# Attention's units reordered to sample, prompt, prompt, with the sample keys turned later and one value load issued earlier

## The reference

```
q = (h @ attn_w_q)                       # 3 groups x 8 heads x 64
for g, (window, dilation) in enumerate(((128, 1), (512, 4), (2048, 16))):
    logits = q[:, :, g] . keys[t - dilation * n] / 8 + bias[g][n]   # n <= window/dilation
    o[g], lse[g] = softmax over n, weighted values
y = merge of the three groups by softmax(lse)  @ attn_w_o
```

## Time and profile before

| what | value |
|---|---|
| median of 3 runs | 2262.54 us (2262.34 to 2266.04) |
| the profiled execution's own time | 2262.11 us |
| its span | 2260.2 us |
| mean granted TensorE clock | 0.992 |
| PE busy | 2214.9 us, 98% |
| DVE busy | 1617.6 us, 72% |
| ACT busy | 890.1 us, 39% |
| DMA, mean over the span | 135 GB/s |

### The profile page before, as it was taken

How to read it: one execution, slowest core, us unless ns; L and a number is a source line. 1 busy time by engine, 2 the same in 40 slices (tenths; PEclk the granted TensorE clock), 3 DMA queues, 4 the chain that set the end, 5 groups by cost and what they waited for, 6 DMA issues and landing times.

```text
span 2260.2 us, 41620 instructions
## 1 busy us (share of the span) xinstructions
PE 2214.9 (98%) x17636; PEld 2102.0 (93%) x17636; DVE 1617.6 (72%) x2138; ACT 890.1 (39%) x1167; POOL 137.3 (6%) x191
## 2 busy tenths in 40 slices
PE   7999999999999999999999999999999999999998
PEld 6999999987799999998889999999987789999998
DVE  7983995699789849953358956984445479947963
ACT  6431443222654314432234422442145555413442
POOL 0000000323010000001001000001001100000001
PEclk8999999999899999999999999999999999999999
DMA  5543443554244435423439533532959933233321
GB/s 156 158 151 110 151 156 93 164 141 126 72 147 150 140 100 164 153 83 90 132 107 304 173 114 99 168 115 73 240 148 281 253 113 94 75 98 96 88 77 55
DMA packets 372091, 305.61 MB, mean 135 GB/s; under 512 B 13798, under 2 KB 338414, under 8 KB 371050
## 3 DMA queue, kind: packets, MB, share of 16 engines
q1 hardware_dynamic: 365485, 232.06, 36.4%
q0 software_dynamic: 6464, 71.76, 9.2%
q10 hardware_dynamic: 12, 0.02, 0.0%
HBM read 284.45 MB, written 70.54 MB: 157 GB/s over the span
## 4 chain that ended last, share of the span: by engine, by line
PE 88%; DVE 6%; issue 2%; ACT 2%; DMA 2%; SPq 1%; DVEq 0%; ACTq 0%
PE ps L2101 34%; PE ps L2157 13%; PE ps L2159 13%; PE ps L2158 13%; PE ps L2565 2%; PE ps L2563 2%; PE ps L2564 2%; PE ps L2401 2%; PE ps L2609 1%; DMA kc<-in_cache_kv_w 1%; DVE blk L1572 1%; PE ps L2725 1%; DVE hlS L1549 1%; PE ps L2663 1%; PE ps L2716 1%
## 5 line engine op out<-in xcount | busy, mean ns | idle before, releaser
L1087 ACT CAST hlS<-blk 128x1024 fp32r<-128x1024 f32 x176 | 184.3, 1053 | 207.0 <-PE ps L2159 169.4
L2101 PE MATMUL ps<-actH,oWA 128*128 128x288 f32 x1408 | 250.4, 296 | 0.0
L2101 PE MATMUL ps<-actH,oWB 128*128 128x288 f32 x1408 | 250.0, 296 | 0.0
L1716 DVE SCALAR_TENSOR_TENSOR cs<-ps,rstd 128x576 f32<-128x576 f32 x64 | 48.5, 757 | 246.9 <-PE ps L2101 246.9
L1549 DVE TENSOR_TENSOR hlS<-blk,hlS 128x1024 fp32r<-128x1024 f32 x176 | 213.5, 1216 | 2.4 <-ACT hlS L1087 2.4
L2157 PE MATMUL ps<-tM,hlA 128*128 128x288 f32 x704 | 212.4, 302 | 2.9 <-DVE hlA L1549 2.4
L2157 PE MATMUL ps<-tE,hlS 128*128 128x288 f32 x704 | 208.5, 296 | 4.1 <-DVE hlS L1549 4.1
L2101 PEld LDWEIGHTS ps<-actH,oWA 128*128 128x128 f32 x1408 | 209.0, 189 | 1.2 <-DVE cs L1611 0.6
L2101 PEld LDWEIGHTS ps<-actH,oWB 128*128 128x128 f32 x1408 | 209.0, 189 | 0.0
L2157 PE MATMUL ps<-tM,hlS 128*128 128x288 f32 x704 | 208.2, 296 | 0.0
L2158 PE MATMUL ps<-tM,hlA 128*128 128x288 f32 x704 | 208.0, 295 | 0.0
(11 more groups left out here) (323 smaller groups left out, 5363.3 us busy)
## 6 DMA issues: line engine op xcount, KB each, us to landing
blk<-in_ffn_w_in SPq DMA_DIRECT2D x352, 256.0 KB, 4.1
raws<-in_ffn_w_out SPq DMA_DIRECT2D x64, 704.0 KB, 4.7
out_kv_sample<-in_cache_kv_w POOLq DMA_DIRECT2D x8, 4064.0 KB, 16.8
out_kv_sample<-in_cache_kv_w POOLq DMA_DIRECT2D x8, 2016.0 KB, 9.2
wst<-in_conv_w_pw SPq DMA_DIRECT2D x24, 512.0 KB, 4.1
wst<-in_w_kv SPq DMA_DIRECT2D x24, 512.0 KB, 3.8
kc<-in_cache_kv_w SPq DMA_DIRECT2D x40, 256.0 KB, 9.1
kc<-in_cache_kv_w SPq DMA_DIRECT2D x8, 1024.0 KB, 7.7
```

The source lines that it names most:

```text
L1087: nc.scalar.copy(o, a).then_inc(S["f_h"], 1)
L1716: nc.vector.scalar_tensor_tensor(px[m % 2], pair(2 + m % 2), 0.5, rstd[:], ALU.mult, ALU.mult).then_inc(S["px_ready"], 1)
L2101: nx = nc.tensor.matmul(outs[t], a, b[:, t, :], start=start and first, stop=stop and b is xh and not first)
```

## The change

- The unit order becomes sample, prompt, prompt: unit i is a sample unit where i % 3 is 0.
- ks (e, 0) is turned two slots ahead of the scores of sample unit e and ks (e, 1) with k0 one slot ahead (before: three, two and one). The loop starts at slot -2.
- The three groups of a pair's keys are turned in one slot, every sixth, which is a sample slot. Before they were spread over three slots.
- SP's waits and issues follow; `pair_bias` and `pair_values` come one slot later in their cycle of six.
- `pair_values(1)` is issued in the query projection instead of slot 2. For that `vinB` is placed in the last 4 blocks of the weight region, which the projection doesn't use.
- Behind the loop ACT waits for all units before it copies half 0, because the last unit is now a prompt unit, whose tokens lie in both halves.

The diff, cut to its core:

```diff
 def prompt_unit(i):
-    return divmod(i // 3 * 2 + i % 3, 4) if i % 3 < 2 else None
+    return divmod(i // 3 * 2 + i % 3 - 1, 4) if i % 3 else None
 def sample_unit(i):
-    return i // 3 if i % 3 == 2 else None
+    return None if i % 3 else i // 3
 def sample_keys_of(s):
-    e, x = divmod(s + 1, 3)
-    return (e, x) if e < NB else None
+    e, y = divmod(s + 2, 3)
+    return (e, y) if e < NB and y < 2 else None
 def prompt_keys_of(s):
-    j, g = divmod(s + 3, 6)
-    return (j, g) if 0 < j < PAIRS and g < 3 else None
+    j, y = divmod(s + 3, 6)
+    return j if 0 < j < PAIRS and y == 0 else None
...
+        pair_values(1)
...
         fresh_values(0)
-        for s in range(-1, UNITS + 3):
+        for s in range(-2, UNITS + 3):
             after = sample_keys_of(s)
             if after and after[0] + 1 < NB:
-                last = ("ks", *after, PAIRS - 1) if after[1] < 2 else ("k0", after[0])
-                sp.wait_ge(S["t_mm"], TURN[last][0] + 1)
+                sp.wait_ge(S["t_mm"], TURN["ks", *after, PAIRS - 1][0] + 1)
                 key_rows(after[0] + 1, after[1])
+                if after[1] == 1:
+                    sp.wait_ge(S["t_mm"], TURN["k0", after[0]][0] + 1)
+                    key_rows(after[0] + 1, 2)
...
-            elif s == 2:
-                pair_values(1)
             kp = prompt_keys_of(s)
-            if kp and kp[1] == 2 and kp[0] + 1 < PAIRS:
-                sp.wait_ge(S["t_mm"], TURN["kp", *kp][0] + 1)
-                pair_keys(kp[0] + 1)
+            if kp and kp + 1 < PAIRS:
+                sp.wait_ge(S["t_mm"], TURN["kp", kp, 2][0] + 1)
+                pair_keys(kp + 1)
...
         act.wait_ge(S["pv_mm"], UNITS - 1)
         split_high(CB["wo"], 0, SIZE["wo"])
-        act.wait_ge(S["o_evac"], UNITS - 1)
+        act.wait_ge(S["o_evac"], UNITS)
+        act.wait_ge(S["t_dve"], TURN["o", NB - 1][2])
         for k in range(PAIRS):
             nc.scalar.copy(oH[:, k, 0], oT[:, k, 0]).then_inc(S["h_h"], 1)
-        act.wait_ge(S["t_dve"], TURN["o", NB - 1][2])
-        act.wait_ge(S["o_evac"], UNITS)
         for k in range(PAIRS):
             nc.scalar.copy(oH[:, k, 1], oT[:, k, 1]).then_inc(S["h_h"], 1)
...
             ks, kp = sample_keys_of(s), prompt_keys_of(s)
-            if ks and ks[1] < 2:
+            if ks:
                 keys_sample(*ks, 0)
                 keys_sample(*ks, 1)
             if 0 <= s - 3:
                 values(s - 3)
-            if ks and ks[1] < 2:
+            if ks:
                 keys_sample(*ks, 2)
                 keys_sample(*ks, 3)
-            elif ks:
+            if ks and ks[1] == 1:
                 keys_dense(ks[0])
             if kp:
-                keys_prompt(*kp)
+                for g in range(3):
+                    keys_prompt(kp, g)
```

More of the change, by code:

```diff
@@ L246, in turn_table @@
         if kp:
-            order.append((("kp", *kp), "act"))
+            order += [(("kp", kp, g), "act") for g in range(3)]
         if 0 <= s - 3 and sample_unit(s - 3) is not None:
@@ L431, in trunk_program @@
                           place("oSs", [P, P]))
+    sbias = place("sbias", [P, SC])
     assert at[0] <= w_at
-    sbias, kTs, kT, vinB, bTB = (place("sbias", [P, SC]), place("kTs", [P, PAIRS, CN]), place("kT", [P, 2, 12, P]),
-                                 place("vinB", [P, 12, P]), place("bTB", [P, 2, PW]))
-    kfT = place("kfT", [P, PAIRS, 2 * FR])
+    at[0] = w_at
+    kTs, kT, bTB, kfT = (place("kTs", [P, PAIRS, CN]), place("kT", [P, 2, 12, P]), place("bTB", [P, 2, PW]),
+                         place("kfT", [P, PAIRS, 2 * FR]))
+    assert at[0] >= w_at + 18 * BLK * 4
+    vinB = place("vinB", [P, 12, P])
     assert at[0] <= w_at + 22 * BLK * 4
@@ L473, in probabilities @@
     def probabilities(i):
-        return sP[i % 3]
+        return sP[i % 3 - 1]
     def slot_column(x, r):
@@ L818, in _ @@
                 fresh_values(1)
-            elif s == 2:
-                pair_values(1)
             kp = prompt_keys_of(s)
-            if kp and kp[1] == 2 and kp[0] + 1 < PAIRS:
-                sp.wait_ge(S["t_mm"], TURN["kp", *kp][0] + 1)
-                pair_keys(kp[0] + 1)
-            if s >= 0 and s % 6 == 4 and s // 6 + 2 < PAIRS:
+            if kp and kp + 1 < PAIRS:
+                sp.wait_ge(S["t_mm"], TURN["kp", kp, 2][0] + 1)
+                pair_keys(kp + 1)
+            if s >= 0 and s % 6 == 5 and s // 6 + 2 < PAIRS:
                 sp.wait_ge(S["sm_ready"], s + 1)
                 pair_bias(s // 6 + 2)
-            if s >= 3 and (s - 3) % 6 == 4 and (s - 3) // 6 + 2 < PAIRS:
+            if s >= 3 and (s - 3) % 6 == 5 and (s - 3) // 6 + 2 < PAIRS:
                 sp.wait_ge(S["pv_mm"], s - 3 + 1)
@@ L1965, in bias_low @@
             else:
-                if i == 2:
+                if i == 0:
                     dve.wait_ge(S["sbias_in"], 16)
@@ L2675, in turn @@
                 if x == 0:
-                    pe.wait_ge(S["pn_ready"], i // 3 * 2 + i % 3 + 1)
+                    pe.wait_ge(S["pn_ready"], i // 3 * 2 + i % 3)
                 out, (_, r), t = bank_for(("p", i, x)), prompt_unit(i), probabilities(i)
```

## The result

The changed kernel takes 2270.03 us, the median of 8 runs (2264.36 to 2274.12), against 2264.91 us for the kernel before in 8 runs beside them (2262.34 to 2266.47). The ratio is 1.0026, with a 95% interval of 1.0017 to 1.0034: slower by some 5 us. The forecast was 2262.6 us and no change, with 2257.5 to 2268.5 as its range.

What follows compares the result with a forecast made beforehand. PE was taken as the bound (88% of the chain), with full DMA engines setting the middle's pace. Terms -0.6 + 2.1 - 1.4 - 1.9 + 2.1 = +0.3 us on 2262.11 gave 2262.6 us, range 2257.5 to 2268.5.

Steps and rivals of the forecast that it cites:

- start: First attention slots: k0's copy wait and its clock go, four smaller costs come; -0.6 us, bounds -1.9 and +0.7.
- middle slots: Middle sample slots: DVE's oSs copy lies bare, probability turns come late, kTs waits go; +2.1 us, bounds +0.5 and +3.5.
- waits for kc: PE's waits for key rows in the middle: 1.0 us instead of 2.4; -1.4 us, bounds -2.4 and +5.
- late instructions: PE's "issue" waits amid full DMA engines, with their clock: 2.7 us instead of 4.6; -1.9 us, bounds -4.6 and +2.
- end: Last units and start of wo: new 2.5 us wait plus clock, less old waits; +2.1 us, bounds -0.3 and +3.
- Two small doubts: At the start: the clock may fall again, 0.7 us; ACT's table load may delay a turn of keys, 0.3 us.
- The slower rival: First prompt slot's keys queue in SP behind pair keys and values, late in slots 7, 13, 19: 2271.9 us, chance 0.2.
- the wait at the squares: Behind wo, squares waiting for ACT behind the next feed-forward's first loads: 1.14 us mostly goes, 0.15 kept.
- The clock behind it: Behind the 2.5 us wait ahead of wo: lowered clock, three in four times 1.6 us, +1.2 us.

Runs made afterwards that it cites:

- thin values: Only 32 of 128 partitions of the 2048-window value rows loaded from sample unit 2 on: 2259.64 us in changed, 2256.84 us in before.
- thin pairs: Changed kernel, with keys of pairs 1 up and values and biases of pairs 2 up loading a quarter of their partitions: 2265.27 us.
- late load: Changed kernel with pair_values(1) issued in slot 2 again, as before: 2269.72 us.
- spread: Changed kernel with the pair values of pairs 2 and 3 issued two slots later, in slots 10 and 16: 2267.82 us.
- thin changed: Changed kernel with a quarter of the 2048-window value rows loaded from sample unit 2 on: 2259.64 us, ratio 0.9979.
- thin before: Kernel before with a quarter of the 2048-window value rows loaded from sample unit 2 on: 2256.84 us, ratio 0.9967.
- the thin pair: The changed kernel and the kernel before, both with the same value rows left out: 2259.64 and 2256.84 us.
- early split: Changed kernel with ACT's split of wo's first chunk two slots earlier: 2273.06, 2269.97 us; 2258.97 with fewer value rows, 2264.55 with sample keys turned as before.
- the best kernel with all its loads: Kernel before with ACT copying k0 ahead of its first exponential in slot 1: 2262.32 us, ratio 0.9992.

## Why the prediction was wrong

The ledger of the two profiled executions, step by step, in us; the measured terms are the waits of the lists above, with what the clock cost behind them:

| step | predicted | measured |
|---|---|---|
| start | -0.6 | -1.6 |
| middle slots | +2.1 | +2.2 |
| waits for kc | -1.4 | -2.4 |
| late instructions | -1.9 | +2.6 |
| end | +2.1 | +3.3 (about +2.1 in the other traces, see below) |
| sum | +0.3 | +4.1 (the executions differ by 4.0) |

**The start** was right in its parts: 0.77 for k0 (said 0.75), 1.53 for the bias (said 1.6). Two small doubts fell the good way: the 1.53 us wait didn't lower the clock (0.7), and no wait followed ACT's table load (0.3). -3.9 + 0.77 + 1.53 = -1.6.

**The middle** was right: four of the five oSs waits of 0.55 and three of 0.25 for kT, less 0.7 for kTs. 2.2 + 0.7 - 0.7 = +2.2.

**The waits for kc**: the profiled execution flatters. Over the traces of the unaltered kernels they are 1.5 us on average after (0, 1.1, 3.5) and 3.2 before (2.4, 4.0): -1.7, near the -1.4 forecast. The slower rival asked for waits of 5 us and more in slots 7, 13 and 19; changed itself shows none such, so the direction it warned of came about by another mechanism.

**The late instructions** are the step that failed: "The DMA stays full for much of the stretch, so I take 2.7 after: -1.9 us". They were taken to shrink with the bytes that left the stretch. The waits went from 3.3 to 5.7 us instead (+2.4), and with the clock the term is +2.6, 4.5 us from the forecast and beyond the upper bound of +2 that I had given it. The clock's part hardly moved: about 1.3 before by the prediction's count, about 1.5 after, where the granted clock is 0.59 at 1748 to 1752. All three traces of the unaltered changed kernel have 5.7 to 5.9 us. What the runs show of the cause:
- It needs full DMA engines: taking bytes away cuts it to 1.9 us (thin values) and 3.4 us (thin pairs) in this order, and to 0.3 in the old order.
- It isn't the early load (late load: 4.8), nor the bunched issues alone (spread: 2.7, but kc 9.1).
- It has a place. Of the waits in slot 12's sample values the profiled execution has 3.3, its repeats 2.5 and 2.5, the late load 3.1 and the thin kernel 1.9 us. Before, the one of 2.4 us stands in the values of a sample unit too.

The traces say what PE waits for. The 18 traces here hold 68 "issue" waits of PE in attention (of more than 0.15 us), and each ends 1.3 to 1.7 us behind the end of a load of 16 KB on DMA queue q8, of the kind "instruction". Counting PE's products and weight loads together, in order, PE resumes each time at a number that differs from the others by a multiple of 256, give or take one (25844, 26100, 26356, 26612, 27123, 27891 and 28403 in changed). Attention has 4836 of them in changed, 18.9 times 256, and 19 of these loads, in every one of the 18 traces. So an "issue" wait is a block of 256 instructions that comes late. The long one, with the block before it and the wait itself (columns as in the earlier trace rows), and then the queues from 1743.5 to 1744.7 (packets, MB, share of 16 engines):

```profile
1737.95:1742.94 4.99, 4.99 (x129) 3.36 (x128) 2.66 (x6) 2.00 (x5) 0.58 (x1) 1.00 1.05 255
1742.94:1746.23 3.29, 0.00 (x1) 0.00 (x0) 0.00 (x0) 0.00 (x0) 0.00 (x0) 1.00 1.07 314
```

```profile
q1 hardware_dynamic: 215, 0.42, 100.0%
q8 instruction: 1, 0.02, 5.6%
```

PE went through the block before (129 products, 128 weight loads) in 4.99 us. The load of the next one started 5.57 us after that block had begun, took 1.07, and PE went on 1.64 us behind it: 8.28 us, less the 4.99 of work, is the wait of 3.29. Over nine blocks of the middle the load starts on average 5.1 to 5.2 us into the block before in the three traces of changed, 4.7 and 4.8 in the two of before, 3.3 and 2.4 in thin changed and thin before. So these loads start late when the engines are full, and nearly as late before as after. With the new order they come some 0.4 us later, and the quickest of the nine blocks takes PE 5.0 us of work instead of 5.5. There are seven such waits in each trace of changed and two in each of before. How much of the +2.4 is the load and how much the quicker blocks isn't separated. The prediction had the term hang on the crowding alone, and left out the other side, how soon PE is through a block. Why a load starts that late is not shown beyond its going with the amount of data; that it queues behind the data is the reading that fits.

**The end**: the wait of 2.46 us was foreseen at 2.5, with its chain, and the wait at the squares went as foreseen. The clock behind it was forecast at 0.75 x 1.6 = 1.2. From the first product of wo to the first one of the squares are 12.37 us, against 9.78 before (1821.40 to 1832.32 less the 1.14 us wait): 2.6 us. The term: 2.5 + 2.46 + 2.6 - 3.1 - 1.14 = +3.3. But the profiled execution is the exception. In the other seven traces with the wait of 2.46 us the same stretch takes 11.1 to 11.25 us, so the clock costs 1.3 to 1.5, as priced, and the term is about +2.1, as forecast. That it came to 2.6 in the one ledger is scatter, and the step did not fail.

**What lies beyond the trace.** The medians differ by 5.1, 7.4 and 3.7 us, the profiled executions by 4.0, at least in part because the changed kernel's traces (2266.0 to 2266.3 us) all come from the faster part of its runs. The order's own part is 2.8 us by the thin pair, from medians, give or take 2. The remaining 1 to 5 us belong to the crowded DMA, by the same pair; their split between kc, "issue" and clock changes from run to run, and I can't give it. I had also centred the forecast on the profiled execution of one kernel, as if the scatter stayed the same; it doubled. Two sums of the prediction are off by a little: 2262.4 plus 0.4 is 2262.8, not 2262.6, and the waits it lists come to 12.0 us, not 11.8. Neither changes the forecast of "no change".

## What to carry to other kernels

Where the trace shows the DMA engines full and PE waiting in the middle of a run without semaphores, an order that takes PE's pauses away doesn't bring the time: price such waits as able to grow when PE's pauses go, and don't let them shrink with a few per cent of bytes. To price one, look for the instruction loads in the list of DMA queues, and compare the time PE takes for the work between two of them with the time from one block's start to the next block's arrival (here 8.28 us against 4.99 at the worst). A wait at the end of a stage costs its length and then the clock: here 1.3 to 1.5 us in seven traces and 2.6 in one, so the usual one goes into the sum and the worst into the bounds. An order with waits for loads should be judged by several traces: waits for copies repeat to 0.1 us, those for loads differ by up to 3.5 us.

## What the runs showed of the hardware

- Waits of 2.46 us ahead of wo lowered the clock in all eight traces that have one, waits of 1.54 us in none of the four (early split). Behind the first kind the products came at half pace for 5.9 us in the profiled execution (24 products, 2.6 us lost, a little more than the wait itself); in the other seven 1.3 to 1.5 us were lost.
- PE's "issue" waits in attention, 68 in 18 traces, all end 1.3 to 1.7 us behind a 16 KB instruction load, at steps of 256 of PE's instructions. These loads start 5.1 to 5.2 us into the block before when the DMA engines are full (three traces of changed), 3.3 with the thin values.
- Leaving the engines a little room was worth more than any reordering tried. The thin values leave out 3/4 of four loads of 256 KB in each of six units, 4.7 MB in all, and the DMA's share in the middle went from 1.08 to 0.92 in before: 7.4 us less, where the best kernel with all its loads lies 2.6 under before, an interval that touches 1.
